# Eight instead of six of sixteen quads with seven products, in pairs, in the output projection of a Trainium2 layer kernel

## The reference, cut to what matters

```python
gates = sigmoid(gate_pre)
o = gates[..., 0:1] * o_cmp + gates[..., 1:2] * o_slc + gates[..., 2:3] * o_win
y_a = o * silu(a_z)
mix = concatenate([y_m, y_a])
x = x + mix @ w_out              # 256x4096 @ 4096x4096
return rmsnorm(x, final_norm_gain)
```

## Time and profile before

| | |
|---|---|
| median of 3 runs | 1789.2 us (1788.47 to 1789.61) |
| profiled execution | 1788.08 us, its span from first to last instruction 1786.1 us |
| granted clock of TensorE, mean | 0.998 of full speed |
| PE busy | 1767.7 us, 99% of the span |
| DVE busy | 1222.4 us, 68% |
| ACT busy | 876.3 us, 49% |
| first stage of two blocks begins on PE | 1483.1 us into the span |

### The profile page before, as it was taken

The page is one execution under the profiler, slowest core; times in us unless marked ns, Lnnn a source line. Parts: engine busy times, 40 slices in busy tenths (PEclk is TensorE's granted clock), DMA queues, the critical chain, the costliest instruction groups (busy, mean ns, idle before and its releaser), DMA issues.

```text
span 1786.1 us, 23230 instructions
## 1 busy us (share of the span) xinstructions
PE 1767.7 (99%) x8142; PEld 1464.7 (82%) x8142; DVE 1222.4 (68%) x1517; ACT 876.3 (49%) x1201; POOL 69.0 (4%) x52
## 2 busy tenths in 40 slices
PE   9999999999999999999999999999999999999997
PEld 7888888888888888888888888888888888888886
DVE  6545644567685767785667566756676877888875
ACT  7545444455555555544444444444444545554653
POOL 0000000001010010100000000000000000000000
PEclk9999999999999999999999999999999999999999
DMA  9656555544445454445555555555555556666675
GB/s 386 236 178 237 178 189 190 187 154 176 153 162 180 148 183 162 168 167 188 189 195 183 179 197 190 189 177 194 195 188 177 188 190 217 214 207 220 223 248 189
DMA packets 97180, 346.94 MB, mean 194 GB/s; under 512 B 10560, under 2 KB 11072, under 8 KB 96704
## 3 DMA queue, kind: packets, MB, share of 16 engines
q1 hardware_dynamic: 94192, 337.22, 54.2%
q10 hardware_dynamic: 2896, 8.39, 1.4%
HBM read 341.38 MB, written 4.19 MB: 193 GB/s over the span
## 4 chain that ended last, share of the span: by engine, by line
PE 94%; DVE 4%; issue 1%; DMA 1%; ACT 0%; DVEq 0%; SPq 0%; POOL 0%; ACTq 0%; POOLq 0%
PE acc_b L562 14%; PE acc_b L564 14%; PE acc_b L563 14%; PE acc_a L562 13%; PE acc_a L563 13%; PE acc_a L564 13%; DVE w_split L1487 1%; PE bank_x L563 1%; PE bank_x L564 1%; PE bank_x L562 1%; PE bank_v L563 1%; PE bank_v L564 1%; PE bank_v L562 1%; DMA w_raw<-in_w_all 1%; PE bank_y L564 1%
## 5 line engine op out<-in xcount | busy, mean ns | idle before, releaser
L1487 DVE TENSOR_TENSOR w_split<-w_raw,w_split 128x1024 fp32r<-128x1024 f32 x579 | 717.0, 1244 | 449.8 <-ACT w_split L1055 447.2
L1055 ACT ACTIVATE w_split<-w_raw 128x1024 fp32r<-128x1024 f32 x579 | 610.6, 1058 | 650.9 <-PE acc_a L564 317.4
L562 PE MATMUL acc_a<-w_split,lhs_hi 128*128 128x512 f32 x1134 | 444.7, 392 | 1.1 <-DVE w_split L1487 1.1
L564 PE MATMUL acc_a<-w_split,lhs_lo 128*128 128x512 f32 x1134 | 441.7, 390 | 0.0
L563 PE MATMUL acc_a<-w_split,lhs_hi 128*128 128x512 f32 x1134 | 441.7, 390 | 0.0
L562 PE MATMUL acc_b<-w_split,lhs_hi 128*128 128x512 f32 x1058 | 416.3, 393 | 0.1
L564 PE MATMUL acc_b<-w_split,lhs_lo 128*128 128x512 f32 x1058 | 412.2, 390 | 0.0
L563 PE MATMUL acc_b<-w_split,lhs_hi 128*128 128x512 f32 x1058 | 411.8, 389 | 0.0
L564 PEld LDWEIGHTS acc_a<-w_split,lhs_lo 128*128 128x128 f32 x1134 | 212.9, 188 | 44.8
L562 PEld LDWEIGHTS acc_a<-w_split,lhs_hi 128*128 128x128 f32 x1134 | 213.0, 188 | 43.3 <-issue 2.6
L563 PEld LDWEIGHTS acc_a<-w_split,lhs_hi 128*128 128x128 f32 x1134 | 213.1, 188 | 40.4
(11 more groups left out here) (384 smaller groups left out, 1407.4 us busy)
## 6 DMA issues: line engine op xcount, KB each, us to landing
w_raw<-in_w_all SPq DMA_DIRECT2D x615, 512.0 KB
wide<-in_x SPq DMA_DIRECT2D x8, 512.0 KB, 9.3
xres<-in_x ACTq DMA_DIRECT2D x8, 512.0 KB, 5.9
out_y<-wide SPq DMA_DIRECT2D x8, 512.0 KB, 3.2
gained_x<-in_x_cols_first SPq DMA_DIRECT2D x2, 1024.0 KB, 10.7
toe<-in_toe_bias ACTq DMA_DIRECT2D x4, 512.0 KB, 5.5
gain_f<-in_final_norm_gain ACTq DMA_DIRECT2D x1, 2048.0 KB, 11.4
gained_x<-in_x_cols_first SPq DMA_DIRECT2D x2, 512.0 KB, 8.2
```

Source lines behind the costliest of these rows:

```text
L562: pe.matmul(dst, a[0], b[0], start=start, stop=False)
L564: return pe.matmul(dst, a[1], b[0], start=False, stop=stop)
L1055: act.activation(w_hi[:, cols], w_raw[:, cols], ACT.Copy).then_inc(hi_done, 1)
L1487: dve.tensor_tensor(w_lo[:, cols], w_raw[:, cols], w_hi[:, cols].bitcast(F32), ALU.subtract).then_inc(lo_done, 1)
```

## The change

In each stage eight quads take seven products, at places 2, 3, 5, 6, 8, 9, 11 and 12, so in four pairs with one eight quad between the pairs. All four weight sums have a place of their own (`t_raw` of 4 blocks): DVE forms t4 directly after t2, before `w_lo` of A; `lo_done` for A comes from `w_lo`; `t_used` becomes `t13_used` (after four of seven products) and `t24_used` (after all). The input sums are formed for eight quads in two halves of four, two operations in a slot, from slot 7 on. The residual is loaded into the place where the result will be (`res`), without `xres`: the first three blocks in slot 14 of the block before the stages, the others two at a time in step 6. ACT's square writes its unused output elsewhere. The sigmoid of the groups stands in slots 19, 22, 25 and 27.

```diff
-SEVEN = tuple(range(6))
-ORDER = (6, 7, 0, 8, 1, 9, 2, 10, 3, 11, 4, 12, 5, 13, 14, 15)
+SEVEN = tuple(range(8))
+ORDER = (8, 9, 0, 1, 10, 2, 3, 11, 4, 5, 12, 6, 7, 13, 14, 15)
-SUM_ORDER, SUMS = (S1, S3, S2, S4), 10
+SUM_ORDER, SUMS, SUM_QUADS = (S1, S3, S2, S4), 7, 4
...
-        t_raw = at("t_raw", Z + 40, 3 * BW)
-        xres = at("xres", Z + 46, 2 * TT * BW)[:, :].rearrange("p (n a c) -> p n a c", n=2, a=TT)
+        t_raw = at("t_raw", Z + 48, 4 * BW)
...
-                pe.wait_ge(a_lo_done, n + 1)
+                pe.wait_ge(lo_done, q + 1)
...
-                passes(shared[P7][:, :], x_sum(S3), w_sum(1), first, final)
+                passes(shared[P7][:, :], x_sum(S3), w_sum(1), first, final).then_inc(t13_used, 1)
...
-                passes(own[0][1][:, :], x_tile(1, 1), w_sum(2), False, False)
-                passes(shared[P6][:, :], x_sum(S2), w_sum(3), first, final).then_inc(t_used, 1)
-            pe.wait_ge(s_lo_done, 1)
+                passes(shared[P6][:, :], x_sum(S2), w_sum(2), first, final)
+                passes(own[0][1][:, :], x_tile(1, 1), w_sum(3), False, False).then_inc(t24_used, 1)
+            pe.wait_ge(s_lo_done, 2)
...
             head(HEADS_M - 1, 3, {c + 2: [lambda c=c: mix_hi(c)] for c in range(MIX_EARLY)},
-                 {SUMS + i: [lambda f=f: input_sums_hi(f)] for i, f in enumerate(SUM_ORDER)})
+                 {SUMS + i // 4 * 4 + j: [lambda k=k: input_sums_hi(k) for k in (i, i + 1)]
+                  for i, j in ((0, 1), (2, 2), (4, 1), (6, 2))})
...
-            def fetch_residual(n, i):
-                act.dma_start(xres[:, i], x_cols[:, :, bass.ds(n * BW, BW)]).then_inc(xr_in[i], 16)
+            def fetch_residual(n, blocks, i):
+                cols = slice(n * BW, (n + blocks) * BW)
+                act.dma_start(res[:, :, cols], x_cols[:, :, cols]).then_inc(xr_in[i], 16)
...
-                if c == 9:
-                    act.wait_ge(ym_done, HEADS_M)
-                    act.wait_ge(s_lo_done, 1)
-                    fetch_residual(0, 0)
+                if c == PAIRS - 2:
+                    act.wait_ge(ht_lo, 2 * PAIRS)
+                    act.wait_ge(s_lo_done, 2)
+                    fetch_residual(0, 1, 0)
+                    fetch_residual(1, 2, 1)
...
                 act.wait_ge(t13_raw, n + 1)
-                act.wait_ge(t_used, n) if n else None
+                if n:
+                    act.wait_ge(t13_used, n)
...
-                act.wait_ge(lo_done, q + 1)
-                act.activation(t_hi[:, 2 * BW:].rearrange("p (i c) -> p i c", i=2),
-                               t_raw[:, :].rearrange("p (i c) -> p i c", i=3)[:, 0:3:2, :],
-                               ACT.Copy).then_inc(t24_hi, 1)
+                act.wait_ge(t4_raw, n + 1)
+                if n:
+                    act.wait_ge(t24_used, n)
+                act.activation(t_hi[:, 2 * BW:], t_raw[:, 2 * BW:], ACT.Copy).then_inc(t24_hi, 1)
...
                     if p < TWOS:
-                        act.wait_ge(seven_free, p)
-                        residuals(p)
+                        fetch_residual(2 * p + 1, 2, 1)
...
-                gate = sigmoid((az_e, g + 1), ebuf, az_r, (18, 20, 22, 24), each=True)
+                gate = sigmoid((az_e, g + 1), ebuf, az_r, (19, 22, 25, 27), each=True)
...
                                   ).then_inc(t2_raw, 1)
+                dve.wait_ge(t2_raw, n + 1)
+                dve.tensor_tensor(sums[:, 3, :], tile(0, 1), sums[:, 2, :], ALU.subtract
+                                  ).then_inc(t4_raw, 1)
                 dve.wait_ge(hi_done, q + 1)
-                weights_lo(0, 0, 2).then_inc(a_lo_done, 1)
+                weights_lo(0, 0, 2).then_inc(lo_done, 1)
...
-                dve.wait_ge(t13_lo, n + 1)
-                dve.wait_ge(t2_raw, n + 1)
-                dve.tensor_tensor(sums[:, 0, :], tile(0, 1), sums[:, 2, :], ALU.subtract
-                                  ).then_inc(lo_done, 1)
```

More of the change, by code:

```diff
@@ L439, in hybrid_layer @@
         t24_lo = sem("t24_lo")
-        t_used = sem("t_used")
+        t13_used = sem("t13_used")
+        t24_used = sem("t24_used")
         x1_copied = sem("x1_copied")
@@ L1434, in two_pieces @@
                 elif r == 29 and p < TWOS:
-                    act.wait_ge(t_used, (p + 1) * len(SEVEN))
+                    act.wait_ge(t24_used, (p + 1) * len(SEVEN))
                     act.activation(x1_copy[:, :], banks(p)[1][P1][:, :], ACT.Copy).then_inc(x1_copied, 1)
@@ L1929, in _, with input_sum @@
             chain.leave(HEADS_M - 1)
-            def input_sum(f):
-                tiles_of = mix_t[:, 0:2 * len(SEVEN), :].rearrange("p (c k) (t q) -> p c k t q", k=2, t=2)
+            def input_sum(i):
+                half, f = i // 4, SUM_ORDER[i % 4]
+                quads = 2 * SUM_QUADS
+                tiles_of = mix_t[:, half * quads:(half + 1) * quads, :].rearrange(
+                    "p (c k) (t q) -> p c k t q", k=2, t=2)
                 a11, a12, a21, a22 = [tiles_of[:, :, k, t, :] for t in range(TT) for k in range(2)]
-                if f == S1:
+                if i == 0:
                     dve.wait_ge(num_ready, HEADS_M)
                     dve.wait_ge(az_free, GROUPS + 1)
+                elif f == S1:
+                    dve.wait_ge(s_lo_done, 1)
                 a, b, op = {S1: (a21, a22, ALU.add), S3: (a11, a21, ALU.subtract),
@@ L1941, in input_sum, with input_sum_lo @@
                 if f in (S2, S4):
-                    dve.wait_ge(s_raw_done, SUM_ORDER.index({S2: S1, S4: S2}[f]) + 1)
+                    dve.wait_ge(s_raw_done, 4 * half + SUM_ORDER.index({S2: S1, S4: S2}[f]) + 1)
                 dve.tensor_tensor(s_raw[:, f], a, b, op).then_inc(s_raw_done, 1)
-            def input_sum_lo(f):
-                dve.wait_ge(s_hi_done, SUM_ORDER.index(f) + 1)
-                last = dve.tensor_tensor(s_lo[:, f], s_raw[:, f], s_hi[:, f].bitcast(F32), ALU.subtract)
+            def input_sum_lo(i):
+                half, f = i // 4, SUM_ORDER[i % 4]
+                dve.wait_ge(s_hi_done, i + 1)
+                part = slice(half * SUM_QUADS, (half + 1) * SUM_QUADS)
+                last = dve.tensor_tensor(s_lo[:, f, part, :], s_raw[:, f],
+                                         s_hi[:, f, part, :].bitcast(F32), ALU.subtract)
                 if f == SUM_ORDER[-1]:
                     last.then_inc(s_lo_done, 1)
-            sums = {SUMS - 2 + i: [lambda f=f: input_sum(f)] for i, f in enumerate(SUM_ORDER)}
-            for i, f in enumerate(SUM_ORDER):
-                sums.setdefault(SUMS + 1 + i, []).append(lambda f=f: input_sum_lo(f))
+            sums = {}
+            for half in range(2):
+                for j, piece in ((0, input_sum), (1, input_sum), (2, input_sum_lo), (3, input_sum_lo)):
+                    sums[SUMS + 4 * half + j] = [lambda i=4 * half + j % 2 * 2 + k, piece=piece: piece(i)
+                                                 for k in range(2)]
             head(HEADS_M - 1, 3, {c + 2: [lambda c=c: mix_lo(c)] for c in range(MIX_EARLY)}, sums)
@@ L1986, in weights_lo @@
                                              ALU.subtract)
-                sums = t_raw[:, :].rearrange("p (i c) -> p i c", i=3)
+                sums = t_raw[:, :].rearrange("p (i c) -> p i c", i=4)
                 for h in range(2):
@@ L2013, in lo_seven @@
                 dve.wait_ge(t24_hi, n + 1)
-                dve.tensor_tensor(t_lo[:, 2 * BW:].rearrange("p (i c) -> p i c", i=2), sums[:, 0:3:2, :],
-                                  t_hi[:, 2 * BW:].bitcast(F32).rearrange("p (i c) -> p i c", i=2),
-                                  ALU.subtract).then_inc(t24_lo, 1)
+                dve.tensor_tensor(t_lo[:, 2 * BW:], t_raw[:, 2 * BW:],
+                                  t_hi[:, 2 * BW:].bitcast(F32), ALU.subtract).then_inc(t24_lo, 1)
             def out_cols(p, h):
@@ L2033, in shared_sums @@
                     dve.tensor_tensor(w, x[P7][:, :], u, ALU.add).then_inc(two_sums_done, 1)
-                    dve.tensor_tensor(res[:, 0, out_cols(p, 1)], u, xres[:, 1, 0, :], ALU.add)
+                    dve.tensor_tensor(res[:, 0, out_cols(p, 1)], u, res[:, 0, out_cols(p, 1)], ALU.add)
                 elif part == 2:
@@ L2037, in shared_sums @@
                     for h in (1, 0):
-                        last = dve.tensor_tensor(res[:, 1, out_cols(p, h)], w, xres[:, h, 1, :], ALU.add)
+                        last = dve.tensor_tensor(res[:, 1, out_cols(p, h)], w, res[:, 1, out_cols(p, h)],
+                                                 ALU.add)
                     last.then_inc(two_sums_done, 1)
```

36 lines of the change are left out of this document (17 added, 19 removed).

## The result

| | before | after |
|---|---|---|
| median of 6 runs each, same chip | 1788.85 us (1788.37 to 1789.61) | 1797.74 us (1796.88 to 1799.94) |
| ratio, 95% interval | | 1.0052 (1.0039 to 1.0065) |
| span of the profiled execution | 1786.1 | 1795.7 |
| granted clock | 0.998 | 0.998 |

The kernel became 8.9 us slower. I had forecast +1.7 us (1790.9) and a range up to 1797.5, so the time lies just above the range.

The account below looks back on a forecast made before the run. The prediction took PE, busy 99%, to bound the kernel, with DVE limiting in the pairs. Terms -4.1 + 4.8 + 2.4 + 2.4 - 3.8 = +1.7 us on 1789.2 gave 1790.9 us; range 1783.5 to 1797.5.

Parts of the forecast that it names:

- What bounds the kernel: PE, busy 99%, bounds the kernel; DVE is slower in a seven quad, which the next eight quad pays back.
- The products: Two more seven-product quads in each of three stages leave out six products of 0.68 us: -4.1 us.
- The order in pairs: Stages: DVE needs 15.60 us per turn against PE's 14.96, so PE stalls 1.6 us a stage: +4.8 us.
- ACT's squares: Second and third stage, step 8: squares make DVE 1.2 us late and PE pays: +2.4 us.
- Weights that land late: Behind pairs, the second slot's load lands 0.35 us late at seven places: +2.4 us, bounds 0 and 5.6.
- The sigmoid's slots: Groups: new slots shorten PE's waits for the sixth and seventh unit's weights: -3.8 us, bounds -5.0 and 0.
- At nothing: Input sums in halves, the residual's load and splitting t_used were priced at zero; a late residual up to 1.5 us.
- PE's restart: In the stages, PE's waking after a wait was counted at 0.05 us a stage, within the pairs' term.
- Rival 2: Behind pairs, transfers bind: second slot 1.0 us late on average, +7.0 instead of +2.4, 1795.5 us; chance 0.20.
- Rivals 1 and 3: 1: DVE keeps up in the pairs, 1783.3 us, chance 0.23; 3: sigmoid slots gain nothing, 1794.7 us, chance 0.11.
- Rival 1: DVE keeps up in pairs; at most 0.3 us and a late 1 us square per stage: 2.0; 1783.3 us; chance 0.23.
- The signs foretold: PE waits 0.3 to 1.5 us in pairs two to four, none in the first; DVE waits for weights behind pairs.

Follow-up runs that it names:

- e3: Changed kernel with every load from the stages on cut to its first half, 256 KB instead of 512, all computing kept: 1789.19 us.
- e10: Changed kernel with weights B rounded and subtracted directly behind A, and ACT's second pair of squares at step 26: 1789.37 us.
- e4: Changed kernel with ACT's second pair of squares in the second and third stage moved from step 8 to step 26: 1796.22 us.
- e8: Changed kernel with weights B rounded and subtracted directly behind A, ahead of t1 and t3, so B's slot is released earlier: 1791.12 us.
- e5: Changed kernel with only the load directly ahead of each late one halved, nine of 96 in the stages: 1792.42 us.
- e1: Kernel before with only the sigmoid moved to slots 19, 22, 25 and 27: 1784.43 us, ratio 0.9978.
- e2: Changed kernel with six quads of seven products in the old alternating order, all else as changed: 1784.39 us, ratio 0.9979.

## Why the prediction was off, point by point

- **What bounds the kernel.** Right: PE was alone on the chain in the stages only because an eight quad paid back what DVE lost in each seven quad. In pairs DVE and the transfers come onto the chain.
- **The products**, -4.1 us: right in count, 18 matmuls.
- **The order in pairs**, +4.8: right. e3 shows 1.67 us in the first stage for 1.6, and 2.8 and 2.7 in the others for 2.8, the squares with them. The first sum starts 1.35 us after the operation ahead of it (1505.30 to 1506.65 on DVE after) where I had 1.26. With it DVE's turn is 15.69 us for 15.60, and PE's turn in e3 is 15.68 (1509.94 to 1525.62).
- **ACT's squares**, +2.4: right in place and size as part of the sum (DVE idle 1.09 for 1.2). Removed without late weights they are worth 2.4 us (e10); e4's 1.0 is too uncertain to say whether late weights lower that.
- **Weights that land late**, +2.4: this step failed, in its size. The seven places were right, each 1.06 us late and not 0.35, so 7.4 us. I had taken 3.1 to 4.0 us from release to landing for B. I came down from the 5.0 of the earlier trace rows because B's release was now 1.7 us behind A's and not 0.6, as if the greater distance came off the landing time. It doesn't: with 0.6 us between the releases, the seven waits of before put B's release to use at 4.3 to 5.2 us, and e8's places at no more than 4.5 to 4.8. With 1.7 us between them it is 4.1 to 4.8. What brings it down is a shorter load ahead: 3.5 to 4.0 us in e5. e3 (-8.1, of which 1.0 is the last block), e5 (-4.9) and e8 (-6.2) each take the wait away in another way. Why B needs about a microsecond more than A (3.4 to 3.6) is only in part shown: some 0.5 us is its later start behind A's data. The Trainium skill, "DMA: Bandwidth & Descriptors", section "Anatomy of one DMA", gives its fit for transfers that GpSimd issues, and here SyncE issues them. By it, as an estimate, B would have landed after 3.2 us and there would have been no wait; the trace has 3.4 to 3.6 us for A and 4.1 to 4.8 for B.
- **The sigmoid's slots**, -3.8: right, 4.2 us in the trace after, 3.9 in e1. The sixth unit lost 0.28 here where I had left 0.30.
- **At nothing**: right for the residual, the input sums and the split of `t_used` (e2 equals e1). The add did not wait. DVE waited 1.7 us for weights at 1483.13, behind the issue of the residual's 1.5 MB, and the lead that the prediction gave covered it; that the residual is the cause is not shown.
- **Not in the sum**: PE's restart, some 1.6 us, and the last block's stalls, 1.0 us. For the restart I had counted 0.05 a stage. It is not a price on top where DVE sets the turn: in e3 the gap of 0.59 and the restart of 0.13 make 0.72 us, which is DVE's turn less PE's, 15.68 - 14.96.
- **The rivals.** Rival 2 was the case, by its mechanism and nearly its price (+7.0 for 7.4). It gave 1795.5; with the 2.6 us that no case held, and the sigmoid's 4.2 for 3.8, -4.1 + 4.8 + 2.4 + 7.4 - 4.2 + 2.6 = +8.9, which is what was measured; the spans differ by 9.6, and those 0.5 to 0.7 us more are what I cannot place. Rivals 1 and 3 fell. Rival 1's 2.0 us was too small by its own terms: 0.3 in three stages and 1 in two are 2.9, so 1784.2 instead of 1783.3. The signs foretold were there: the nine waits of PE, none listed in the first pair (0.2 us in the second and third stage), the first sum behind an eight quad late. PE's gaps reached 1.9 us, where I had 0.3 to 1.5.

## What to carry to other kernels

When two transfers are released shortly after one another, price the second by measured rows of a second one, and do not take it down towards the first because the releases lie farther apart. Then look at which operation of the consumer releases it: here moving one short operation forward was worth more than the products that the change saved. An engine that runs level with PE turns each delay upstream into PE's time, so count every one of them again, at the same price, when slack is taken away. Try the parts of a change alone: one number, the sigmoid's slots, was its whole gain.

## What the runs showed of the hardware that I had not expected

- A 512 KB load behind another: 3.4 to 3.6 us from release to use for the first, 4.1 to 4.8 for the second, released 1.7 us later (changed kernel). Released only 0.6 us later, the second took at most 4.5 to 4.8 (e8). With half the bytes in the first, the second took 3.5 to 4.0 (e5). The DMA engines were idle for 1.0 us after the first release.
- A matmul that follows a wait of PE is itself followed after 0.34 us, not 0.227, though the granted clock stays at 0.998.
- Idle time that the profile puts down to "issue", 7.4 us in seven places, was a transfer: with half the bytes it was gone (e3).
